# First mixer of a two-block model: another order of projection units, the inverse started by substitution on VectorE

## The reference

```python
qkv = causal_conv_silu(proj[..., P:P + 3 * G], conv_w[l])
qh = l2_norm(heads(q)) * (Dh ** -0.5)
kh = l2_norm(heads(k))
g = -jnp.exp(a_log) * jax.nn.softplus(a + dt_bias)
kb = kh * beta[..., None]
m = jnp.einsum('bhncd,bhnjd->bhncj', kb, kh) * decay_strict
lhs = jnp.eye(C, dtype=f32) + m
sol = lax.linalg.triangular_solve(lhs, rhs, left_side=True, lower=True)
...
v_new = val - jnp.einsum('bhcd,bhde->bhce', kc, state)
o = jnp.einsum('bhcd,bhde->bhce', qd, state) + jnp.einsum('bhcj,bhje->bhce', ai, v_new)
...
mix = jnp.concatenate([pool_out, gdn_out], axis=-1)
h = h + mix @ w_out[l]
```

## Time and profile before

| | |
|---|---|
| Median of 3 executions | 1176.15 us (1172.94 to 1179.1) |
| The profiled execution | 1177.17 us, span 1175.4 us |
| TensorE busy | 1098.7 us, 93% of the span |
| VectorE, ScalarE, GpSimd busy | 720.2, 550.3, 46.5 us |
| Mean granted TensorE clock | 0.975 |

### The profile page before, as it was taken

How to read it: one execution, slowest core, us unless ns; L and a number is a source line. 1 busy time by engine, 2 the same in 40 slices (tenths; PEclk the granted TensorE clock), 3 DMA queues, 4 the chain that set the end, 5 groups by cost and what they waited for, 6 DMA issues and landing times.

```text
span 1175.4 us, 20755 instructions
## 1 busy us (share of the span) xinstructions
PE 1098.7 (93%) x8770; PEld 1064.4 (91%) x8770; DVE 720.2 (61%) x979; ACT 550.3 (47%) x656; POOL 46.5 (4%) x40
## 2 busy tenths in 40 slices
PE   5896688999999999999999999999699999999997
PEld 4886678999999879999999999998589899999997
DVE  2664534744546778766655566889966657544553
ACT  3456323634344555535444445796544316444441
POOL 0102310000000000000000000032000000000000
PEclk9998789999999999999999999999899999999999
DMA  9243212555575365555655554514100034655521
GB/s 294 82 140 108 72 36 72 172 189 178 178 271 196 128 195 179 189 169 179 215 176 181 181 177 126 180 37 158 58 1 1 22 123 150 223 188 188 182 72 36
DMA packets 116960, 167.51 MB, mean 143 GB/s; under 512 B 5792, under 2 KB 97568, under 8 KB 116512
## 3 DMA queue, kind: packets, MB, share of 16 engines
q1 hardware_dynamic: 115184, 166.18, 43.7%
q10 hardware_dynamic: 1712, 0.43, 0.2%
HBM read 165.55 MB, written 1.05 MB: 142 GB/s over the span
## 4 chain that ended last, share of the span: by engine, by line
PE 80%; DVE 12%; issue 3%; ACT 3%; DMA 1%; POOL 0%; SPq 0%; DVEq 0%; ACTq 0%; POOLq 0%
PE banks L1874 22%; PE banks L1876 22%; PE banks L1875 22%; DVE sb_w_low L1145 2%; ACT sb_w_high L637 1%; PE banks L2302 1%; PE banks L2379 1%; DVE sb_arena L1215 1%; PE banks L2367 1%; DVE sb_arena L1735 1%; DMA sb_constants<-in_constants 1%; DVE sb_state L1732 1%; PE banks L2010 1%; PE banks L2017 1%; PE banks L2182 1%
## 5 line engine op out<-in xcount | busy, mean ns | idle before, releaser
L1145 DVE TENSOR_TENSOR sb_w_low<-sb_raw,sb_w_high 128x2048 fp32r<-128x2048 f32 x150 | 344.9, 2303 | 274.3 <-ACT sb_w_high L637 274.2
L1874 PE MATMUL banks<-sb_act_high,sb_w_low 128*128 128x256 f32 x1376 | 396.3, 288 | 16.4 <-DVE sb_arena L1204 5.9
L637 ACT ACTIVATE sb_w_high<-sb_raw 128x2048 fp32r<-128x2048 f32 x150 | 285.6, 1910 | 268.4 <-PE banks L1876 268.3
L1876 PE MATMUL banks<-sb_act_high,sb_w_high 128*128 128x256 f32 x1376 | 391.7, 285 | 0.0
L1875 PE MATMUL banks<-sb_act_low,sb_w_high 128*128 128x256 f32 x1376 | 389.1, 283 | 0.0
L1874 PEld LDWEIGHTS banks<-sb_act_high,sb_w_low 128*128 128x128 f32 x1376 | 261.7, 190 | 21.6 <-DVE sb_arena L1204 7.5
L1875 PEld LDWEIGHTS banks<-sb_act_low,sb_w_high 128*128 128x128 f32 x1376 | 264.2, 192 | 0.4 <-issue 0.2
L1876 PEld LDWEIGHTS banks<-sb_act_high,sb_w_high 128*128 128x128 f32 x1376 | 260.8, 190 | 0.0
L1874 PE MATMUL banks<-sb_hidden_high,sb_w_low 128*128 128x256 f32 x896 | 254.2, 284 | 0.6 <-DVE sb_hidden_low L1558 0.6
L1876 PE MATMUL banks<-sb_hidden_high,sb_w_high 128*128 128x256 f32 x896 | 253.5, 283 | 0.0
L1875 PE MATMUL banks<-sb_hidden_low,sb_w_high 128*128 128x256 f32 x896 | 251.3, 280 | 0.0
(11 more groups left out here) (341 smaller groups left out, 1169.6 us busy)
## 6 DMA issues: line engine op xcount, KB each, us to landing
sb_raw<-in_ffn_w SPq DMA_DIRECT2D x64, 1024.0 KB, 5.3
sb_raw<-in_w_up SPq DMA_DIRECT2D x16, 1024.0 KB, 5.3
sb_raw<-in_w_down SPq DMA_DIRECT2D x16, 1024.0 KB, 5.0
sb_raw<-in_sgu_w_in SPq DMA_DIRECT2D x16, 1024.0 KB, 5.3
sb_raw<-in_rwkv_w_rkv SPq DMA_DIRECT2D x12, 1024.0 KB, 5.5
sb_raw<-in_w_in SPq DMA_DIRECT2D x10, 1024.0 KB, 6.9
sb_raw<-in_sgu_w_out SPq DMA_DIRECT2D x8, 1024.0 KB, 5.0
sb_raw<-in_w_out SPq DMA_DIRECT2D x4, 1024.0 KB, 5.2
```

The source lines that it names most:

```text
L637: nc.scalar.activation(whi[s][:], raw[s][:], ACT.Copy).then_inc(hi_done, 1)
L1145: nc.vector.tensor_tensor(wlo[s][:], raw[s][:], f32(whi[s][:]), ALU.subtract).then_inc(lo_done, 1)
L1874: nc.tensor.matmul(dst, l_lo, r_hi, start=start, stop=False, **kw)
L1876: return nc.tensor.matmul(dst, l_hi, r_hi, start=False, stop=stop, **kw)
```

## The change

The units of w_in come in the order keys, queries, pooled, values, gate. The constants (now 640 columns smaller) are loaded behind unit 2, and the ones are a memset. The squares of x are two VectorE products, and the gate matmuls stand behind unit 1. The key products, decays and L are made after unit 2.

The inverse starts from diagonal blocks of 32x32: ScalarE packs the 32 blocks into `MX.D`, VectorE transposes them, and substitutes 15 steps on both halves (16x16 blocks) at once; a transpose and four copies spread the result. Levels 4, 5 and 6 remain for TensorE. Their groups (`turn_wt`, `left_level`, `right_level`) stand between quarters of units 6, 7 and 8 (`part(j, n)`, 12 matmuls), and the steps of the recurrence between quarters of unit 9. The query products are made there too. The w_out units first multiply the four pooled rows, all four of them, and then the four others.

```diff
-LEVELS = 7
+LEVELS = (4, 5, 6)
...
-    ident, ones = cmat("ident"), cmat("ones")
+    ident, ones = cmat("ident"), sb("ones", [P, P])[:, :]
+    level_mask = lambda l: cmat("levels", LEVELS.index(l))
...
+    MX.L = [carve(10328, 8, P), carve(12376, 8, P), MX.LT]
...
+    MX.B, MX.Wb = over_hid[:, 0:1024], arena[:, 12376:13400]
+    MX.D, MX.E = over_hid[:, 1024:2048], over_hid[:, 1024:2048]
+    MX.W, MX.X = (over_hid[:, 1024 * i:1024 * i + 1024].rearrange("p (a b) -> p a b", b=P) for i in range(2))
+    in_blocks = lambda v: v.rearrange("p (a b) -> p a b", b=32)
+    halves_of = lambda v: v.rearrange("p (s r) -> p s r", s=2)[:, :, 0:512].rearrange("p s (a b) -> p s a b", b=32)
+    MX.B16, MX.W16 = halves_of(over_hid[:, 0:1056]), halves_of(arena[:, 12376:13432])
...
-    IN_COLS = [4, 5, 2, 3, 6, 7, 0, 1, 8, 9]
+    IN_COLS = [4, 5, 2, 3, 0, 1, 6, 7, 8, 9]
+    CONV_UNITS = [0, 1, 2, 3, 6, 7]
+    OUT_BANKS = [4, 5, 2, 3]
...
-            if j == 0:
+            if j == 2:
...
+        chain.add(pool.memset(MX.Wb, 0.0))
+        pool.memset(MX.D, 0.0).then_inc(blocks_set, 1)
+        chain.settle()
+        pool.memset(MX.Wb[:, ::33], 1.0).then_inc(blocks_set, 1)
         pool.wait_ge(cm_in, 16)
         pool.wait_ge(decay_done, 2)
-        pool.tensor_tensor(MX.AT[:], MX.ET[:], cmat("upper").rearrange("p (a b) -> p a b", a=1)
-                           .broadcast_to([P, 8, P]), ALU.mult).then_inc(decay_mask, 1)
-        pool.wait_ge(decay_mask, 1)
-        pool.tensor_tensor(MX.ET[:], MX.ET[:], over(cmat("neg_upper_strict"), 8), ALU.mult)\
-            .then_inc(decay_mask, 1)
-        def inversion(call, LT, LTl):
-            pool.wait_ge(lt_ready, 2 * call + 2)
-            for l in range(1, LEVELS):
-                n = 12 * call + 2 * (l - 1)
-                if n:
-                    pool.wait_ge(inv_x_ps, n)
-                pool.tensor_tensor(LTl[:], LT[:], over(cmat("levels", l), 8), ALU.mult).then_inc(inv_lt, 1)
-        pool.wait_ge(proj_out, 8)
-        pool.wait_ge(kqn_done, 4)
+        pool.tensor_tensor(MX.AT[:], MX.ET[:], over(cmat("upper"), 8), ALU.mult).then_inc(decay_mask, 1)
+        pool.wait_ge(lt_ready, 2)
+        pool.wait_ge(kqn_done, 2)
+        pool.tensor_tensor(MX.L[0][:], MX.LT[:], over(level_mask(4), 8), ALU.mult).then_inc(inv_lt, 1)
+        pool.wait_ge(mx_base, 1)
+        pool.tensor_tensor(MX.L[1][:], MX.LT[:], over(level_mask(5), 8), ALU.mult).then_inc(inv_lt, 1)
+        pool.wait_ge(mx_diag, 1)
+        pool.wait_ge(inv_lt, 2)
+        pool.tensor_tensor(MX.L[2][:], MX.LT[:], over(level_mask(6), 8), ALU.mult).then_inc(inv_lt, 1)
+        pool.wait_ge(proj_out, 6)
+        pool.wait_ge(gsum_ps, 3)
...
+        def silu(i):
+            act.wait_ge(conv_done, 2 * i + 2)
+            kq = MX.qkv[:, 2 * i:2 * i + 2, :]
+            nc.scalar.activation(kq, kq, ACT.Silu).then_inc(silu_done, 1)
+            if i < 4:
+                act.wait_ge(silu_done, i + 1)
+                nc.scalar.activation(MX.sq[:, 2 * i:2 * i + 2, :], kq, ACT.Square).then_inc(sq_done, 1)
...
+        high(2)
+        first_tap(0)
+        silu(0)
+        high(3)
+        first_tap(1)
+        silu(1)
+        log_exp()
...
+        scale_of(0)
+        scale_of(1)
+        high(4)
+        high(5)
+        first_tap(2)
...
+        high(6)
+        act.wait_ge(blocks_set, 2)
+        act.wait_ge(lt_ready, 2)
+        for b in range(4):
+            rows = slice(32 * b, 32 * b + 32)
+            last = nc.scalar.activation(in_blocks(MX.D)[rows, :, 0:8].rearrange("p i n -> p n i"),
+                                        MX.LT[rows, :, 32 * b:32 * b + 32], ACT.Copy)
+        last.then_inc(mx_diag, 1)
+        first_tap(3)
+        high(7)
+        high(8)
+        act.wait_ge(mx_base, 1)
+        act.wait_ge(cm_in, 16)
+        for b in range(4):
+            last = nc.scalar.activation(MX.WT[:, :, 32 * b:32 * b + 32],
+                                        in_blocks(MX.E)[:, :, 0:8].rearrange("p i n -> p n i"), ACT.Copy,
+                                        scale=cm[:, CMATS["quads"][0] + b:CMATS["quads"][0] + b + 1])
+        last.then_inc(mx_wide, 1)
+        high(9)
+        take_w(0)
+        silu(2)
+        take_x(0)
+        silu(3)
+        take_w(1)
+        first_tap(4)
+        take_x(1)
+        silu(4)
+        take_w(2)
+        first_tap(5)
+        take_x(2)
+        silu(5)
         log_exp()
-        high(9)
-        for j in range(4):
-            act.wait_ge(ss_done, 2 + j)
-            rsqrt_of_sums(MX.sq[:, 2 * j:2 * j + 2, :], two(bank[2 + j][:]), 1.0).then_inc(r_done, 1)
+        scale_of(2)
+        scale_of(3)
...
+            nc.scalar.activation(MX.Vt[:, 4 * m:4 * m + 4, :], bank[2 + m][:].rearrange("p (a b) -> p a b", a=4),
+                                 ACT.Copy).then_inc(tr_done, 1)
...
+        nc.vector.memset(ones, 1.0)
...
+        for h in range(2):
+            hs = slice(4 * h, 4 * h + 4)
+            dve.wait_ge(x_in[h], 16)
+            last = nc.vector.tensor_tensor(MX.sq[:, hs, :], x[:, hs, :], x[:, hs, :], ALU.mult)
+        last.then_inc(sq_done, 1)
...
+        dve.wait_ge(edges_set, 1)
+        take_pre(0)
+        taps(0)
+        low(3)
+        take_pre(1)
+        taps(1)
...
+        take_pre(2)
+        low(4)
+        taps(2)
+        for m in range(CH):
+            dve.wait_ge(decay_done, m + 1)
+            dve.wait_ge(gsum_ps, m + 1)
+            ms = slice(4 * m, 4 * m + 4)
+            chain.add(nc.vector.tensor_tensor(MX.LT[:, ms, :], MX.ET[:, ms, :], over(cmat("neg_upper_strict"), 4), ALU.mult))
...
+            chain.settle(chain.n - 1 + m)
...
+                lt = MX.LT[:, 4 * m + h, :]
+                last = nc.vector.scalar_tensor_tensor(lt, bank[2 + m][:, h * P:h * P + P], s[5][:, m, h:h + 1], lt,
+                                                      ALU.mult, ALU.mult)
+        low(5)
+        take_pre(3)
+        low(6)
+        dve.wait_ge(mx_diag, 1)
+        chain.add(nc.vector.transpose(MX.B, MX.D))
+        chain.settle()
+        for j in range(15):
+            shape = [P, 2, 15 - j, j + 1]
+            tmp = MX.part[:, 0:2 * shape[2] * shape[3]].rearrange("p (s a b) -> p s a b", s=2, b=j + 1)
+            below = MX.W16[:, :, j + 1:16, 0:j + 1]
+            chain.add(nc.vector.tensor_tensor(tmp, MX.B16[:, :, j + 1:16, j:j + 1].broadcast_to(shape),
+                                              MX.W16[:, :, j:j + 1, 0:j + 1].broadcast_to(shape), ALU.mult))
+            chain.settle()
+            chain.add(nc.vector.tensor_tensor(below, below, tmp, ALU.add))
+            chain.settle()
+        nc.vector.transpose(MX.E, MX.Wb).then_inc(mx_base, 1)
+        take_pool(4)
+        take_pool(5)
+        low(7)
+        taps(3)
+        add_level(0)
+        take_pre(4)
+        low(8)
...
+        add_level(1)
+        taps(4)
+        take_pre(5)
+        taps(5)
+        add_level(2)
+        low(9)
+        normalise(2)
+        normalise(3)
+        take_z(8)
...
+        def quarter(u, b, n):
+            s = u % RING
+            h, l = (w[s][:, :].rearrange("p (k n) -> p k n", k=KT) for w in (whi, wlo))
+            if n == 0:
+                pe.wait_ge(lo_done, u + 1)
+            t = n // 2
+            cs = slice(t * P, t * P + P)
+            for k in range(4 * (n % 2), 4 * (n % 2) + 4):
+                ins = split_matmul(bank[b][:, t * T:t * T + T], h[:, k, cs], l[:, k, cs], act_hi[:, k, :],
+                                   act_lo[:, k, :], start=k == 0, stop=k == KT - 1)
+            if n == 3:
+                ins.then_inc(w_used, 1)
...
+        take(0)
+        take(1)
         pe.wait_ge(ab_col, 2)
...
+        norms(0)
+        norms(1)
+        take(2)
+        pe.wait_ge(kqn_done, 2)
+        products(0, 2)
...
+        take(3)
+        take(4)
...
+        take(5)
...
+        def turn_wt(l):
+            for h in range(2):
+                if l == 0:
+                    pe.wait_ge(mx_wide, 1)
+                else:
+                    pe.wait_ge(inv_wt, 2 * (l - 1) + h + 1)
+                    pe.wait_ge(inv_x, 2 * (l - 1) + h + 1)
+                for q in range(4):
+                    last = nc.tensor.transpose(bank[2 + h][:, q * P:q * P + P], MX.WT[:, 4 * h + q, :], ident)
+                last.then_inc(inv_t_ps, 1)
+        def left_level(l):
+            pe.wait_ge(inv_lt, l + 1)
+            for h in range(2):
+                pe.wait_ge(inv_w, 2 * l + h + 1)
+                for q in range(4):
+                    last = nc.tensor.matmul(bank[2 + h][:, q * P:q * P + P], MX.L[l][:, 4 * h + q, :],
+                                            MX.W[:, 4 * h + q, :], start=True, stop=True)
+                last.then_inc(inv_x_ps, 1)
+        def right_level(l):
+            if l == 0:
+                pe.wait_ge(decay_done, 2)
+            for h in range(2):
+                pe.wait_ge(inv_x, 2 * l + h + 1)
+                for q in range(4):
```

(62 more changed lines are left out.)

497 lines of the change are left out of this document (213 added, 284 removed).

## The result

| | before | after |
|---|---|---|
| Median of 4 executions | 1176.16 us (1172.94 to 1179.1) | 1126.09 us (1125.15 to 1127.84) |
| Span of the profiled execution | 1175.4 us | 1124.1 us |
| Mean granted TensorE clock | 0.975 | 0.986 |

The ratio is 0.9577, 95% interval 0.9549 to 0.9604: 50 us less, where the prediction's sum gave 44.9. Behind the mixer nothing changed: the first activation of the MLP's hidden units starts at 214.77 us before and at 163.63 after, 51.1 earlier, and the spans differ by 51.3.

What follows compares the result with a forecast made beforehand. TensorE's path through the first mixer was taken as the bound: its stages, waits and 2.0 us of handoffs summed to 162.8 against 207.7, 44.9 less, so 1177.2 became 1132 us; range 1120 to 1149.

Steps and rivals of the forecast that it cites:

- Start: TensorE to unit 2's end: sums from 9.8 us, unit 0 at 15.6, unit 1 ends 27.6, unit 2 ends 45.1.
- Wait: TensorE ahead of unit 6: idle 68.7 to 75.6, 6.9 us, until VectorE copies unit 4 out after the substitution.
- lock: VectorE instructions with two SBUF inputs and GpSimd ones reading SBUF exclude one another: 2.1 + 1.7 us added before the substitution.
- substitution: VectorE's 15 steps of two instructions, 0.22 to 0.33 us each, mean 0.29: 8.7 us for 30.
- blocked price: Rival: the substitution's operations cost 30 x 0.69 us in place of 8.7, +12, 1144 us; chance 0.10.
- the price of a unit: TensorE's projection units: 48 matmuls, 6.0 us each, from a unit running 33.27 to about 39.2.
- the small groups: TensorE's three inversion levels: transposes 1.3, left 2.0, right 1.9 us each, 15.6 together.
- the 2.0 us for queues that I couldn't see: Handoffs between engines on the mixer's path: 0.4 us counted, unseen queues on top; 2.0 taken, between 0.4 and 5.
- Late trips: Rival: level round trips lose cover behind Silu, taps, low halves; six, 2 to 3 us late: 1144 to 1150; chance 0.15.
- Lower clock: Rival: short groups hold TensorE's clock at half from 75 to 160 us, +62, 1194 us; chance 0.03.
- No change: Rival: mixer ends early but the FFN's units are not there; the 45 us come back, 1177; chance 0.02.
- Better than the sum: Rival: no lock (3.8), quick restarts (3), handoffs at 0.4 (1.6): 1124 us; chance 0.10.

Runs made afterwards that it cites:

- The two runs on the start: Changed kernel with constants loaded behind unit 0 and awaited by the sum of squares: 1128.6 us; changed kernel with gate matmuls ahead of unit 0: 1136.25 us.
- the unbroken levels: Changed kernel with units 6 and 7 whole, then three levels with no projection between, then unit 8: 1137.99 us.
- the versions with the units first: Changed kernel, units 6 and 7 whole beside the substitution, unit 4 copied before it, levels among unit 8's quarters: 1122.44 us; three more versions add edits.
- the decay mask alone later: Units 6 and 7 whole under the substitution, plus GpSimd's decay mask moved behind the pooled sums, first level mask unmoved: 1124.89 us.
- the units of w_out whole: Changed kernel with w_out's unit 0 taking its four pooled rows first, the other units run one after another: 1133.47 us.
- both masks later as well: Units 6 and 7 whole under the substitution, plus decay mask behind the pooled sums and first level mask behind the substitution: 1128.09 us.
- the copy first: Changed kernel with VectorE copying unit 4 out ahead of the substitution: 1126.15 us.
- the masks later: Changed kernel with GpSimd's decay mask behind the pooled sums and first level mask behind the substitution: 1123.78 us.

## Why the prediction was right, and where its 6 us are

The path was followed step by step. Predicted and measured:

| Point on TensorE's path | predicted | measured |
|---|---|---|
| first matmul | 9.8 | 8.29 |
| unit 0 starts; unit 1 ends | 15.6; 27.6 | 15.51; 27.28 |
| unit 2 ends | 45.1 | 45.5 |
| unit 5 ends | 68.7 | 68.14 |
| unit 6 starts (the wait) | 75.6 (6.9) | 74.60 (6.46) |
| levels and unit 8 end | 113.2 | 110.7 |
| outputs end | 133.5 | 129.9 |
| last W_out matmul ends | 159.4 | 154.67 |
| MLP runs without a gap, as if from | 162.8 | 156.4 |

The last line is the start at 157.83 less the 12 matmuls (1.44 us) that ran between the three short stalls. It is 6.4 below the sum: 51.3 in the spans against 44.9.

- **Start: right within 0.4 us, in part by luck.** Memset ones, squares on VectorE, gate matmuls behind unit 1. The first matmul came 1.5 us earlier than predicted, but the sums took 6.3 in place of 5.8 and unit 0 waited 0.95. The sum priced the gate matmuls and unit 2 at their long form, and the profiled execution had it; eight other versions were 1.5 to 2 us shorter there. The two runs on the start show that the order matters more than the earlier first matmul: 2.5 us for the constants, 10 for the gate matmuls.
- **Wait, lock and substitution: right.** 30 operations of 0.19 to 0.29 us with 0.03 between, 64.03 to 72.7 = 8.7 us, as summed; the blocked price of 0.66 has no row. The lock cost 2.1 (4.60 against 2.46) and 1.6 (3.88 against 2.29), where 2.1 and 1.7 stood in the sum; leaving the operations out removed the wait, and moving the masks took 3.8 off it. The restart cost 1.9 (24 matmuls in 4.79 us, against 24 x 0.12 = 2.88), where I took 1.7.
- **Mis-sized: the price of a unit, 6.0 us.** That was the first start to the last end of one unit, with the tail of its last matmul. Back to back the tail lies under the next: 11.77 us for two units, so 48 x 0.12 = 5.76 each, and 0.24 less for each of the 14: 3.4 us.
- **Mis-sized: the small groups.** Transposes, left and right were priced 1.3, 2.0 and 1.9; the steps to the next instruction are 0.87, 1.78 and 1.78. In three levels that is 2.3 us. Again the tail: in a queue that goes on it is not paid. The chain that ended last gives the net price at once; this is its part for one level, with the wait and the first group of the next:

```profile
88.13 0.87 PE banks L2085 x8
...
90.44 1.78 PE banks L2093 x16
...
93.66 1.80 PE banks L2103 x16
...
99.12 0.58 ACT sb_over_hidden L693
...
99.84 2.02 PE banks L2093 x16
```

- **Not there: the 2.0 us for queues that I couldn't see.** They were added on top of handoffs priced one by one. Against it stand waits that the sum had smaller or not at all: 2.24 at the step in place of 1.7, 0.65 (the copy at 99.12, behind six taps) and 0.78 in the middle in place of 0.4, and the three stalls of the MLP's start at 1.7 with their tails in place of 1.4. In the table, the middle is 1.5 us shorter than predicted, the end 1.1 and W_out 1.1. So the three terms come to 7.7 us, the larger waits take back 1.9, and of the 6.4 some 0.6 stay unexplained. One sign named for being right was missed by this: the last W_out matmul ended at 154.67, ahead of the 158 to 166.
- **The rivals.** *Late trips* is what the unbroken levels give: 12 us. In the changed kernel only the one wait of 0.65 is of that kind. *Lower clock*: from 74.6 to 110.6 the grant is 0.95, from 110.6 on 1.00; here short groups with quarters between kept it. The Trainium skill, "TensorE: Matmul & The Clock Gate", HAM oscillation, warns of idle gaps; the trace agrees in the one place with a long gap (1.9 us of slow restart behind 6.46 us). Behind shorter gaps the rows of this case go both ways: 2.6, 2.7 and 2.9 us of waiting were followed by slow groups, while behind the 2.24 us of the changed kernel the products took 1.95, at full clock (last section). *No change* needed the MLP's units to be late; they were there. *Better than the sum* named no lock, quick restarts and no unseen queues; only the last of them happened, and what made the time better was a term that it did not have.

What stays open: how the 51 us divide between fewer levels and better cover. Up to the start of the MLP (207.7 us before, 156.7 after), TensorE is idle 28 us less (48.5 against 20.2) and busy 23 less (159.2 against 136.5). Three levels fewer are at the priced groups of the earlier trace rows 3 x 4.4 = 13 of the 23. The rest fits the higher granted clock, 0.95 on average in place of 0.90, but no run shows that by itself, and none had the old six levels in the new order. Of the parts of the change, the runs price the order of the gate matmuls (10 us), the quarters between the levels (12) and the split of W_out (7); these are losses from taking one part away, and need not add up.

## What to carry to other kernels

Price a group in a full queue by the distance between starts, the tail once at the end of a stretch; and add nothing for queues unseen on top of handoffs already counted. When a wait of the bound engine ends with a copy, look one wait further: if the data behind it is as late, only work that fills the time helps, not the copy's place. And look at each long instruction in front of a short one that the bound engine waits for: moving one low half of 2.3 us was worth 3.2. Before moving work away from a chain, see what the chain waits for next: in the versions with the units first it was unit 4's end, 0.8 us away.

## What the runs showed of the hardware

- **The place where the clock falls differs between the profiled executions, with the same matmuls in front.** The 48 gate matmuls begin at full clock behind unit 1, with steps of 0.11 us, and in all versions but one go over to 0.21 at some point; in the one with the decay mask alone later they end at full clock, and the norms and unit 2 behind them begin slow. In the changed kernel's timeline of TensorE:

```profile
30.39 0.25 PE L1954 MATMUL banks<-sb_ab_high,sb_act_low 128*128 128x8 f32 x1
...
30.64 0.36 PE L1956 MATMUL banks<-sb_ab_high,sb_act_high 128*128 128x8 f32 x1
30.85 0.35 PE L1954 MATMUL banks<-sb_ab_high,sb_act_low 128*128 128x8 f32 x1
```

  The stretch took 7.07 us here, and 6.19, 8.14, 5.41 and 6.29 in the four versions with the units first, with the same instructions in front. Unit 2 behind it took 7.22, and 6.50, 6.25, 6.96 and 6.45. Of the eleven versions with the gate matmuls in this place, three took 14.3 to 14.4 us for the two together (the changed kernel, the units of w_out whole, both masks later as well) and eight 12.4 to 12.8. That is 1.5 to 2 us that no edit explains, as much as some of the effects sought; I had held this stretch for a fixed price. TensorE had no gap there: what went before the fall from 2.4 to 1.2 GHz was matmuls of 8 columns.
- **The same wait is or is not followed by the lower clock.** In eight versions TensorE waits 2.23 or 2.24 us ahead of the second step of the recurrence. From its end to the first matmul of W_out are 12.1 us in five of them and 13.6 to 13.7 in three (the copy first, the masks later, the levels unbroken), with the same instructions between; behind the wait of 2.60 us it was 13.5 to 13.7 in all three versions that have it. A gap of 2.74 us ahead of unit 6 was followed by 24 matmuls in 4.57 us, nearly the 4.79 behind 6.46 us.
- **GpSimd is held as much as it holds.** Its product of 128x1024 takes 2.40 us alone and 4.38 when it starts 0.16 us behind a low half of VectorE. The two then alternate, so that a second VectorE instruction pays as well (3.88 us).
- **Small operations of VectorE with four-dimensional operands** cost 0.19 us at 30 elements and 0.29 at 128, with 0.03 to the dependent next one: fifteen elimination steps for 8 systems are 8.7 us, less than two levels on TensorE with their round trips (5.15 each). The two transposes around them, 1.2 us each, and ScalarE's copies come on top.
